# First compression layer of two neighbouring blocks from three products instead of two times two, in the decode passes of a hybrid decoder step

## The reference, cut to what matters

```python
CMP_BLOCK = 32; CMP_STRIDE = 16; CMP_HIDDEN = 128; HEAD_DIM = 64; NSA_KV_HEADS = 2
def compress_rows(rows, pos_emb, w1, w2):
    nc = (L - CMP_BLOCK) // CMP_STRIDE + 1                      # 127 blocks of 2048 rows
    idx = jnp.arange(nc)[:, None] * CMP_STRIDE + jnp.arange(CMP_BLOCK)[None, :]
    blk = rows[:, idx] + pos_emb[None, None, :, None, :]
    blk = jnp.swapaxes(blk, 2, 3).reshape(B, nc, NSA_KV_HEADS, CMP_BLOCK * HEAD_DIM)
    return jax.nn.gelu(blk @ w1) @ w2                           # 2048 -> 128 -> 64
# per layer and sequence:
kcmp = rms_norm(compress_rows(kc_full, cmp_pos, cmp_w1_k, cmp_w2_k), kc_norm)
vcmp = compress_rows(vc_full, cmp_pos, cmp_w1_v, cmp_w2_v)
```

## Time and profile before

| what | value |
|---|---|
| median of 3 runs | 1865.57 us (1865.45 to 1867.22) |
| the profiled execution | 1868.04 us, span 1866.3 us |
| TensorE busy | 1838.7 us (99% of the span) |
| VectorE busy | 1204.6 us (65%) |
| ScalarE busy | 372.3 us (20%) |
| GpSimd busy | 119.1 us (6%) |
| passes of the first layer start (L908) at | 306.4, 341.2, 374.9, 411.8 us |

### The profile page before, as it was taken

The page is one execution under the profiler, slowest core; times in us unless marked ns, Lnnn a source line. Parts: engine busy times, 40 slices in busy tenths (PEclk is TensorE's granted clock), DMA queues, the critical chain, the costliest instruction groups (busy, mean ns, idle before and its releaser), DMA issues.

```text
span 1866.3 us, 27349 instructions
## 1 busy us (share of the span) xinstructions
PE 1838.7 (99%) x10438; PEld 1412.1 (76%) x10438; DVE 1204.6 (65%) x2676; ACT 372.3 (20%) x957; POOL 119.1 (6%) x218
## 2 busy tenths in 40 slices
PE   8999999999999999999999999999999999999999
PEld 7767777877777777777777676777777777777777
DVE  5899796442667677673268997954427667676631
ACT  2013375322100100000001134842211000100000
POOL 1011400110000000000000114001000000000000
PEclk9999999999999999999999999999999999999999
DMA  7302564663112222131242044057431212222111
GB/s 276 129 1 88 161 209 157 214 221 111 57 68 72 87 68 90 58 136 63 80 152 79 1 122 143 1 182 249 161 122 45 90 69 80 78 70 109 72 62 51
DMA packets 110390, 199.86 MB, mean 107 GB/s; under 512 B 13393, under 2 KB 81250, under 8 KB 105266
## 3 DMA queue, kind: packets, MB, share of 16 engines
q1 hardware_dynamic: 90946, 161.87, 25.5%
q0 software_dynamic: 5488, 29.93, 4.6%
q10 hardware_dynamic: 13824, 6.30, 1.3%
HBM read 190.36 MB, written 15.94 MB: 111 GB/s over the span
## 4 chain that ended last, share of the span: by engine, by line
PE 94%; DVE 4%; ACT 1%; issue 1%; DMA 0%; POOL 0%; DVEq 0%
PE ps L1065 30%; PE ps L1130 15%; PE ps L755 12%; PE ps L616 8%; PE ps L651 8%; PE ps L603 7%; PE ps L859 2%; PE ps L822 2%; PE ps L841 2%; PE ps L999 1%; PE ps L659 1%; PE ps L893 1%; PE ps L908 1%; PE ps L695 1%; PE ps L862 1%
## 5 line engine op out<-in xcount | busy, mean ns | idle before, releaser
L2140 DVE TENSOR_TENSOR xT<-xT,ps 128x288 f32<-128x288 f32 (+3 forms) x55 | 41.7, 758 | 153.2 <-PE ps L1130 152.9
L1065 PE MATMUL ps<-catT,rD 128*128 128x288 f32 x528 | 131.6, 406 | 0.0
L1065 PEld LDWEIGHTS ps<-catT,rD 128*128 128x128 f32 x528 | 100.3, 190 | 27.7
L1497 ACT ACTIVATE rD<-rD 128x592 f32<-128x592 f32 x44 | 30.7, 697 | 450.2 <-DVE rD L2082 450.2
L755 PE MATMUL ps<-WR,rD 128*128 128x254 f32 (+1 forms) x512 | 120.2, 382 | 0.2
L1065 PE MATMUL ps<-catT,XC 128*128 128x288 f32 x480 | 119.8, 406 | 0.4 <-DVE rD L2054 0.4
L1065 PE MATMUL ps<-rA,WR 128*128 128x288 f32 x448 | 117.8, 406 | 0.0
L1065 PEld LDWEIGHTS ps<-catT,XC 128*128 128x128 f32 x480 | 91.0, 190 | 26.2 <-issue 1.2
L755 PEld LDWEIGHTS ps<-WR,rD 128*128 128x128 f32 x512 | 93.0, 188 | 18.6 <-issue 2.9
L1065 PEld LDWEIGHTS ps<-rA,WR 128*128 128x128 f32 x448 | 85.1, 190 | 23.5
L616 PE MATMUL ps<-catT,WR 128*128 128x288 f32 x384 | 98.8, 410 | 2.0 <-ACT catT L1231 1.1
(11 more groups left out here) (376 smaller groups left out, 3317.7 us busy)
## 6 DMA issues: line engine op xcount, KB each, us to landing
WR<-in_w_up SPq DMA_DIRECT2D x56, 512.0 KB, 3.7
WR<-in_kvc SPq DMA_DIRECT2D x128, 128.0 KB, 2.3
rB<-in_w_up SPq DMA_DIRECT2D x32, 512.0 KB, 4.3
rD<-in_kvc SPq DMA_DIRECT2D x96, 128.0 KB
rD<-in_w_down SPq DMA_DIRECT2D x8, 1408.0 KB, 7.6
rB<-in_ksT SPq DMA_DIRECT2D x160, 64.0 KB, 4.0
rB<-in_w_down SPq DMA_DIRECT2D x6, 1408.0 KB, 6.0
WR<-in_w_glu SPq DMA_DIRECT2D x16, 512.0 KB, 3.9
```

What stands on the lines that cost most here:

```text
L1065: ins = mm(ps[:, bank, 0:HN], w[:, k, :], h[:, k, :], start=k == 0, stop=k == 3)
L2140: step(tt(x, x, src, ALU.add))
```

## The change

Blocks m = 2k and 2k+1 share a chunk. With even chunks e(k) and odd chunks o(k), the code now makes three products of 128 columns (64 pairs, two heads), each the sum of 8 products of a 128x128 weight: first = B e, second = A o, third = (A+B)(e+o). Then hidden(2k) = third - first - second and hidden(2k+1) = second(k) + first(k+1).

On TensorE `third(i, part)` takes the place of `half(i)`: 24 products with 128 columns instead of 16 with 254. GpSimd adds e+o in place over the even chunks (`row_sums`), once part 0 has read them. VectorE makes A+B once per layer at the end of `prompt` (`weight_sums_of`, into YB, causal and the tail of XC). ScalarE copies the three results from PSUM to SBUF (`thirds_kept`), and VectorE joins them there (`gelu_in_joined`: five instructions in place of three). Since the three results fill columns 0 to 383 of a bank, and bank 7 holds window scores there, TensorE waits for `cmp_max` ahead of the other work of each pass, pass 3 too. Two transfers of a later layer (the history into XC and the mask into causal) move behind the decode passes on SyncE.

```diff
             def key_rsqrt(nb): ...
+            def row_sums(b, n):
+                pool.wait_ge(*count("hb_made"))
+                rows = kvc[rows_at(b)][:, 0:32 * PAST // CHUNK].rearrange("p (m q e) -> p q m e", q=2, e=32)[:, :, :, 16 * n:16 * (n + 1)]
+                pool.tensor_tensor(rows[:, 0], rows[:, 0], rows[:, 1], ALU.add).then_inc(sh["hs_made"], 1)
...
                     if p + 1 < NPR:
+                        for job, b, n, c, bank in HALVES[p]:
+                            row_sums(b, n)
                         key_rsqrt(NCS)
                         key_rsqrt(NCS)
...
-                    def half(i, js=range(16)):
+                    def third(i, part, js=range(NPAIR)):
                         job, b, n, c, bank = HALVES[p][i]
-                        hidden(l, job, b, n, js=js, bank=bank, taken=...)
+                        if part == 0 and js[0] == 0:
+                            if n == 0:
+                                pe.wait_ge(*count(f"kv_in{rows_at(b)}", 256))
+                            if i == 2:
+                                pe.wait_ge(sh["hb_kept"], 9 * l + 3 * p + 1)
+                            elif p:
+                                pe.wait_ge(sh["hb_kept"], 9 * l + 3 * p - (0 if i == 0 else 1))
...
+                        if part == 2 and js[0] == 0:
+                            pe.wait_ge(sh["hs_made"], 9 * l + 3 * p + i + 1)
...
+                        for j in js:
+                            o = n * 16 + j * 2
+                            w = (w1[n][:, NPAIR + j, :], w1[n][:, j, :], wab[n][j])[part]
+                            ins = mm(thirds(bank)[part], w, rows[:, :, o:o + 2], start=j == 0, stop=j == NPAIR - 1)
+                    pe.wait_ge(*count("cmp_max"))
                     if more:
-                        half(0)
+                        third(0, 0)
+                        third(0, 1)
+                        third(1, 0)
+                        third(0, 2)
...
-                        half(1)
-                        half(2, range(9) if p < 2 else range(16))
+                        third(1, 1)
+                        third(1, 2)
+                        third(2, 0)
+                        if p < 2:
+                            third(2, 1, range(4))
+                        else:
+                            third(2, 1)
+                            third(2, 2)
...
+                    def thirds_kept(i):
+                        act.wait_ge(sh["hid_made"], 16 * l + 8 + 3 * p + i)
+                        if 3 * p + i:
+                            act.wait_ge(sh["hx_made"], 9 * l + 3 * p + i)
+                        bank = HALVES[p][i][4]
+                        copy(kept[0], ps[:, bank, 0:2 * P])
+                        copy(kept[1], ps[:, bank, 2 * P:3 * P]).then_inc(sh["hb_kept"], 1)
...
                     if more:
-                        tanhed(tanh[0], NCS)
-                        fetch_keys(range(8, 16))
+                        thirds_kept(0)
+                        fetch_keys(range(7, 13))
                     act.wait_ge(*count("s_masked"))
                     act.activation(S[:, 0:2056], S[:, 0:2056], ACT.Exp, ...)
                     if more:
+                        tanhed(tanh[0], NCS)
+                        thirds_kept(1)
                         tanhed(tanh[1], NCS)
...
                     ins.then_inc(sh["s_kept"], 1)
                     if p < 2:
+                        thirds_kept(2)
                         tanhed(tanh[2], NCS)
...
+            def gelu_in_joined(n, s, bank):
+                dve.wait_ge(*count("hb_kept"))
...
+                step(tt(even, first, second, ALU.add))
+                stt(odd, second[:, 0:63], posb[:, n:n + 1], first[:, 1:64], ALU.add, ALU.add)
+                stt(even, third, posb[:, n:n + 1], even, ALU.add, ALU.subtract).then_inc(sh["hx_made"], 1)
+                dve.wait_ge(*count("hx_made"))
+                step(stt(g, x, 0.044715, x, ALU.mult, ALU.mult))
+                stt(g, g, 1.0, x, ALU.add, ALU.mult).then_inc(sh["cmp_in"], 1)
...
                 count("pt_made", sum(BANKS[t] for g, t in STEPS[13:]))
+                weight_sums_of(1)
+                dve.wait_ge(sh["uc_out"], 16 * (l + 1))
+                weight_sums_of(0)
```

More of the change, by code:

```diff
@@ L303, in counter, with each_other, thirds @@
             return seen_of, count
+        def each_other(ap, at, m):
+            return bass.AP(ap.tensor, ap.offset + 2 * at, [list(ap.ap[0]), [4, m], [1, 2]])
+        def thirds(bank):
+            return [ps[:, bank, P * i:P * (i + 1)].rearrange("p (m h) -> p m h", h=2) for i in range(3)]
         def rows_at(b):
@@ L926, in decode @@
                     more = p + 1 < NPR
[L928 removed]
+                    def third(i, part, js=range(NPAIR)):
                         job, b, n, c, bank = HALVES[p][i]
[L930 to L931 removed]
+                        if part == 0 and js[0] == 0:
[5 more added lines that the diff above has]
+                                pe.wait_ge(sh["hb_kept"], 9 * l + 3 * p - (0 if i == 0 else 1))
+                            elif i == 0:
+                                pe.wait_ge(sh["cmp_in"], 16 * l + 7)
+                        if part == 2 and js[0] == 0:
+                            pe.wait_ge(sh["hs_made"], 9 * l + 3 * p + i + 1)
+                            if p == 0:
+                                pe.wait_ge(sh["ab_made"], 2 * l + 2 - n)
+                        rows = kvc[rows_at(b)][:, 0:32 * PAST // CHUNK].rearrange("p (m q e) -> p q m e", q=2, e=32)[:, 1 if part == 1 else 0]
+                        for j in js:
+                            o = n * 16 + j * 2
+                            w = (w1[n][:, NPAIR + j, :], w1[n][:, j, :], wab[n][j])[part]
+                            ins = mm(thirds(bank)[part], w, rows[:, :, o:o + 2], start=j == 0, stop=j == NPAIR - 1)
+                        if js[-1] == NPAIR - 1 and part != 1:
+                            ins.then_inc(sh["hid_made" if part else "hb_made"], 1)
                     def first_left(k0, K):
@@ L980, in decode @@
                         if p < 2:
-                            half(2, range(9, 11))
+                            third(2, 1, range(4, 8))
                         else:
@@ L1005, in decode @@
                         if j == 5 and p < 2:
-                            half(2, range(11, 12))
+                            third(2, 2, range(1))
                         if j == 5 and p == 2:
@@ L1010, in decode @@
                             if p < 2:
-                                half(2, range(12, 14))
+                                third(2, 2, range(1, 3))
                             else:
@@ L1015, in decode @@
                             if p < 2:
-                                half(2, range(14, 15))
+                                third(2, 2, range(3, 5))
                             keys_second(l, 2 * p + 4, NCS, sample_pick, CG[cb])
@@ L1027, in decode @@
                         if p < 2:
-                            half(2, range(15, 16))
+                            third(2, 2, range(5, 8))
                         else:
@@ L1432, in decode @@
                     if more:
[L1433 removed]
+                        fetch_keys(range(7))
                     act.wait_ge(*count("pct_made"))
@@ L1915, in decode @@
                     tt(y, y, thl, ALU.mult).then_inc(sh["conv_done"], 1)
-                    halves_of = [(n, NCS, c) for job, b, n, c, bank in HALVES[p]]
-                    banks_of = [bank for job, b, n, c, bank in HALVES[p]]
                     if p == 0:
                         gelu_out(0, NCS, late[0][3])
-                    if more:
-                        gelu_in(*halves_of[0], banks_of[0])
-                    else:
+                    if not more:
                         dve.wait_ge(*count("left_made"))
```

48 lines of the change are left out of this document (35 added, 13 removed).

## The result

The changed kernel takes 1890.99 us (median of 4 runs, 1889.39 to 1895.38), the kernel before 1866.39 us on the same chip (4 runs, 1865.45 to 1868.71). The ratio is 1.0134 with a 95% interval from 1.0121 to 1.0147: 25 us slower, where +10 was forecast and 1886 was the range's end. The profiled executions span 1888.6 and 1866.3 us, 22.3 apart.

What follows compares the result with a forecast made beforehand. The prediction took TensorE's work and waits to bound the kernel, with the selected-score chain the next limit. Saving -29.7, waits +29.2 and GpSimd's additions +10.7 gave +10.2 us, so 1875.8 us, range 1860 to 1886.

Steps and rivals of the forecast that it cites:

- in no stretch but the two there were: Expected sign in the profile after: TensorE's clock at half rate only in the two stretches that already had it.
- a rival at 0.2: Three to seven TensorE clock drops to 1.2 GHz behind long waits, 1881 to 1888 us; chance 0.2.
- saving on TensorE: First-layer pieces: 48 records at 0.112 us replace 32 at 0.219, 1.65 us a piece, 29.7 us in both layers.
- wait 1: Start of each pass: TensorE waits for VectorE's cmp_max, 1.57 us, twice 2.55, net 0.6 in pass 3; 14.6 us.
- wait 2: Before the turns: shorter filling uncovers the exponential, 0.8 us in each of two passes, 3.2 us in both layers.
- wait 3: Before the second layer's value product: ScalarE's copies of turned weights come late, 11.4 us in both layers.
- GpSimd's additions: Passes 0 to 2: the 2.2 us addition for piece 2 stops VectorE, 1.8 us six times, 10.7 us.
- clock falls: TensorE drops from 2.4 to 1.2 GHz after idling, up to 1.7 us lost each; not in the forecast's sum.
- Rival A: GpSimd and VectorE do not stop each other, or the addition falls beside VectorE's work: 1865 us; chance 0.2.
- Rival C: ScalarE's queue is shorter, so wait 3 and GpSimd's stop of VectorE fall away: 1854 us; chance 0.12.

Runs made afterwards that it cites:

- e5: The changed kernel with idle products of fitted length in TensorE's waits for cmp_max and for the copied turned weights; 1877.60 us, ratio 1.0047.
- e2: The changed kernel with GpSimd adding 2 columns of one chunk instead of 16 x 32 x 2; 1874.98 us, ratio 1.0035.
- e7: The kernel before with the changed kernel's wait for cmp_max ahead of each pass's first piece, pass 3 too; 1879.59 us, ratio 1.0061.
- e8: e6 with TensorE's order rewritten for three products, importance product right behind the first thirds, no cmp_max wait in pass 3; 1870.72 us, ratio 1.0011.
- e12: e11 with ScalarE's key transfers spread, GpSimd's first addition behind conv_done and some TensorE products shifted; 1873.15 us, ratio 1.0027.
- e4: The changed kernel with the cmp_max wait behind two thirds of piece 0 and no such wait in pass 3; 1880.87 us, ratio 1.0061.
- e10: e6 with the first key norm ahead of piece 1 on VectorE and ScalarE, key transfers behind ScalarE's copies; 1888.17 us, ratio 1.0113.
- e3: The changed kernel with ScalarE copying three of five turned banks of weights before piece 1; 1899.61 us, ratio 1.0178.
- e6: The changed kernel with all five turned-weight copies before pieces 1 and 2, pass 2's early output projection parts later; 1897.74 us, ratio 1.0157.
- e11: e8 with the key norm ahead of piece 1 and key transfers behind the copies, as in e10; 1870.66 us, ratio 1.0015.

## Why the prediction was wrong

The direction, the places of the waits and most of their sizes were right. The total was wrong by one step, the sentence that PEclk would be at 0.5 "in no stretch but the two there were": the sum has the clock at nothing and keeps its falls as a rival at 0.2. The runs showed ten falls, 15.0 us.

Measured for both layers, in us (waits from the lists above; "remainder" means that it was not measured by itself):

| step | forecast | measured |
|---|---|---|
| saving on TensorE | -29.7 | -27.7 (start to start: L755 128.4 before, L966 100.7 in e5) |
| wait 1, `cmp_max` | +14.6 | +13.7 (12.4, and pass 3 longer by 2 x 0.65) |
| wait 2, exponential | +3.2 | +2.2 |
| wait 3, copies | +11.4 | +7.5 (e2: 6.8, and 0.7 more at L1046) |
| GpSimd's additions | +10.7 | +11.1 (after against e2: the stop 9.6, TensorE's own wait 1.5) |
| not taken apart | 0 | +2.5, remainder |
| sum | +10.2 | +9.3 (passes, e5 against before) |
| clock falls | 0 | +15.0 (after against e5, behind each wait) |
| start of pass 0, pass 3 | 0 | -1.2 (after against e5) |
| the passes | +10.2 | +23.1 |

- **Saving.** 1.54 us a piece instead of 1.65. The pace was near the forecast: 0.115 us a record in the rows of pass 0, for 0.112.
- **Wait 1.** 1.44, 2.37 and 2.39 us for 1.57, 2.55 and 2.55, and pass 3 is longer by 0.65 for a net 0.6. e7 shows that such a wait counts in full.
- **Wait 2.** 0.55 us in two passes for 0.8.
- **Wait 3.** Without additions 0.87, 0.88 and 1.66 us in the three passes, plus 0.18 behind the first two. The queue on ScalarE was counted too long by 0.8 us, and by 0.4 in pass 2.
- **GpSimd.** The addition took 2.34 to 2.40 us for an estimated 2.2, and it stopped VectorE as the earlier trace rows suggested from the other side. Rival A (no stop) falls with the rows of L1832. In pass 2 TensorE also waited 0.74 us for the sum itself, which has no term in the prediction.
- **The clock.** The case was in view in the earlier trace rows: 1.31 us busy in a stretch, then one at 0.50. The prediction made three to seven falls of it, with a chance of 0.2, because idle times of 1.4 to 1.7 us "did not always do it". That was true (e7: one fall behind eight waits of 1.3 to 1.5 us) and beside the point: six waits of the forecast itself were 3.6 to 3.9 us long with the stop in them, and four 2.55. All ten came, at 2.4 to 2.9 us, and each has its fall. Ten falls at the measured 1.5 us on top of the forecast are 1875.8 + 15 = 1890.8, and 1891.0 was measured. That the agreement is this close is luck in part: the terms above are off by up to 4 us each and cancel. All ten was not certain either, since e2 has two waits of 2.4 us without a fall.
- **Rival C** (the saving stands) failed: its turning point, piece 1 joined before the turns begin, was missed by 4.6 us in pass 0 (turns from 325.84, piece 1 joined at 330.40), and even the orders made for it (e8 to e12) came only to the time of before.

## What to carry to other kernels

On an engine that is 99% busy, a shortened product can uncover the chain that it had covered, as all three waits here show: price the waits together with the saving, and the long ones with the clock fall that can stand behind them (1.5 us each, shown by e5). In the changed kernel all ten waits of 2.4 to 2.9 us had one, in e2 two of four of 2.4 us, and single waits of 3.2 us (e4, 1291.40) and 3.4 us (e10, 412.03) had none. To split waits from clock, fill the waits with idle products of fitted length; count the records, not the products. A wait is taken off by its whole chain, not by its last instruction: in e3, e6 and e10 each swap on ScalarE only handed 1.3 to 3.4 us to the next consumer.

## What the runs showed of the hardware

- GpSimd's addition stops more than VectorE's sums of two tensors. In e11 a product of one SBUF tensor with a number per row waited as well; the same instruction in the changed kernel, with GpSimd idle, comes second:

```profile
314.13 2.37 POOL L523 TENSOR_TENSOR rD<-rD 128x1024 f32<-128x1024 f32 x1 [2.99 <-PE ps L966]
...
314.43 2.16 DVE L2002 TENSOR_SCALAR rA<-rA,st 128x127 f32<-128x127 f32 x1
```

```profile
311.39 0.28 DVE L2000 TENSOR_SCALAR rA<-rA,st 128x127 f32<-128x127 f32 x1
```

In e12 one of 32 columns did too, while a copy from PSUM, the maxima and the replacement ran through beside two additions (314.84 to 319.67). The last row is the stopped one; it takes 0.18 us where GpSimd is idle (382.26):

```profile
316.82 0.19 DVE L2015 COPY impv<-ps 128x30 f32<-128x30 f32 x1 [1.74 <-PE ps L997]
317.05 0.20 DVE L2017 MAX8 impv<-impv 128x8 f32<-128x33 f32 x1
...
317.88 0.18 DVE L2020 MATCH_REPLACE8 MX<-impv 128x33 f32<-128x33 f32 x1
318.10 1.62 DVE L2021 TENSOR_SCALAR MX<-MX 128x32 f32<-128x32 f32 x1
```

The Trainium skill has this in SBUF — State Buffer (Who interferes with whom): a `tensor_scalar` from SBUF to SBUF can enter a mode that takes the ports shared with GpSimd too, and whoever comes second stands for the whole instruction of the other. The traces of e11 and e12 agree (0.28 to 2.16 us, 0.18 to 1.62 us); the prediction had used only the part on two inputs.
